# High products ahead of low ones behind seven norms, an output chunk inside the way back, and four moved steps, in a two-block transformer kernel

## The reference, cut to what matters

```python
def modulate(x, g_pre, shift, scale):
    return rms_norm(x, g_pre) * (1 + scale) + shift
def residual_add(x, y, g_post, gate, res_w):
    return x + res_w * (1 + gate) * rms_norm(y, g_post)
# first block, for each of two layers: mod = silu(c) @ ada_w + ada_b
x = residual_add(x, swiglu(modulate(x, ...), gate, up, down), ...)    # d_ff 2816
x = residual_add(x, token_mixer(modulate(x, ...), ...), ...)          # three attentions, gated sum, @ w_out
x = residual_add(x, swiglu(modulate(x, ...), gate, up, down), ...)
# second block, for each of two layers: mod = silu(c_2) @ ada_w_2 + ada_b_2
h = rms_norm(x) * (1 + sc1) + sh1
x = x + g1 * attention(h)          # layer 0: differential ("heads a"), layer 1: chunked band ("heads b")
h = rms_norm(x) * (1 + sc2) + sh2
x = x + g2 * grouped_moe(h)        # 16 experts of width 512, two per token
```

## Time and profile before

| | |
|---|---|
| median of 3 runs | 2142.19 us (2140.47 to 2143.39) |
| profiled execution, its own time | 2136.77 us |
| its span, first to last instruction | 2135.0 us |
| PE busy | 1974.8 us, 92% |
| DVE busy | 1413.3 us, 66% |
| ACT busy | 849.8 us, 40% |
| mean granted TensorE clock | 0.979 |

### The profile page before, as it was taken

One profiled execution on the slowest core, in us unless ns is written; L12 is line 12 of the kernel. 1 busy time (PEld: TensorE's weight loads), 2 busy tenths in 40 slices (PEclk: granted clock), 3 DMA queues, 4 the chain that ended last, 5 costly groups with the idle time before them and its releaser, 6 DMA issues.

```text
span 2135.0 us, 25771 instructions
## 1 busy us (share of the span) xinstructions
PE 1974.8 (92%) x9588; PEld 1440.6 (67%) x9588; DVE 1413.3 (66%) x2138; ACT 849.8 (40%) x1127; POOL 62.9 (3%) x95
## 2 busy tenths in 40 slices
PE   3999999998999999999998999998799989879998
PEld 2788777776887788778776788776544447654443
DVE  6899787766897789877876789786411146742112
ACT  3343555555343543454665444564200035321000
POOL 0000000000000000000000000110000001000000
PEclk9999999999999999999999999999899989889999
DMA  9999544436897699654443799652999986259997
GB/s 397 374 366 376 183 175 155 152 120 246 337 366 290 270 367 375 249 187 158 157 146 140 313 371 378 195 219 91 327 421 421 421 322 249 103 204 419 421 421 318
DMA packets 98175, 597.87 MB, mean 280 GB/s; under 512 B 20240, under 2 KB 23696, under 8 KB 27408
## 3 DMA queue, kind: packets, MB, share of 16 engines
q1 hardware_dynamic: 91600, 585.18, 70.4%
q10 hardware_dynamic: 6464, 11.15, 1.5%
HBM read 595.21 MB, written 1.09 MB: 279 GB/s over the span
## 4 chain that ended last, share of the span: by engine, by line
PE 74%; DVE 10%; DMA 6%; ACT 5%; issue 3%; POOL 1%; SPq 0%; DVEq 0%; ACTq 0%
PE acc L2313 11%; PE gu L2661 10%; PE acc L2317 10%; PE acc L2316 10%; PE gu L2313 7%; PE gu L2317 7%; PE gu L2316 7%; PE tr L2661 6%; PE tr L2411 3%; PE acc L2661 3%; DMA proj<-ada_stream 2%; DVE w_lo L1361 2%; ACT w_hi L699 2%; DMA stage<-wstream 2%; DMA more_proj<-wstream 1%
## 5 line engine op out<-in xcount | busy, mean ns | idle before, releaser
L1361 DVE TENSOR_TENSOR w_lo<-stage,w_hi 128x2048 fp32r<-128x2048 f32 x232 | 530.3, 2289 | 81.5 <-ACT w_hi L699 80.3
L699 ACT ACTIVATE w_hi<-stage 128x2048 fp32r<-128x2048 f32 x232 | 442.6, 1912 | 218.8 <-PE acc L2317 213.4
L2313 PE MATMUL acc<-w_hi,hT_hi 128*128 128x512 f32 (+1 forms) x736 | 305.5, 415 | 20.1 <-DVE hT_lo L2179 12.4
L1426 DVE SCALAR_TENSOR_TENSOR proj<-proj,c_row 128x1024 f32<-128x1024 f32 x240 | 291.9, 1220 | 41.5 <-DMA proj<-ada_stream 30.1
L2313 PE MATMUL gu<-w_hi,hT_hi 128*128 128x512 f32 x704 | 282.7, 402 | 21.7 <-DVE pair L1496 10.5
L2317 PE MATMUL acc<-w_hi,hT_lo 128*128 128x512 f32 (+1 forms) x736 | 291.0, 395 | 0.0
L2316 PE MATMUL acc<-w_lo,hT_hi 128*128 128x512 f32 (+1 forms) x736 | 290.5, 395 | 0.0
L2316 PE MATMUL gu<-w_lo,hT_hi 128*128 128x512 f32 x704 | 277.0, 394 | 0.0
L2317 PE MATMUL gu<-w_hi,hT_lo 128*128 128x512 f32 x704 | 277.0, 393 | 0.0
L2313 PE MATMUL acc<-w_hi,yT_hi 128*128 128x512 f32 (+1 forms) x460 | 180.9, 393 | 3.3 <-ACT proj L1141 2.7
L2313 PEld LDWEIGHTS acc<-w_hi,hT_hi 128*128 128x128 f32 x736 | 141.3, 192 | 57.9 <-DVE hT_lo L2179 15.9
(11 more groups left out here) (256 smaller groups left out, 2333.8 us busy)
## 6 DMA issues: line engine op xcount, KB each, us to landing
stage<-wstream SPq DMA_DIRECT2D x312, 1024.0 KB, 5.6
proj<-ada_stream SPq DMA_DIRECT2D x120, 1024.0 KB, 7.8
w_raw<-wstream SPq DMA_DIRECT2D x72, 1024.0 KB, 19.3
z_mix<-wstream SPq DMA_DIRECT2D x12, 1024.0 KB, 16.6
more_yT<-wstream SPq DMA_DIRECT2D x12, 1024.0 KB, 17.9
more_prob<-wstream SPq DMA_DIRECT2D x12, 1024.0 KB, 17.6
more_proj<-wstream SPq DMA_DIRECT2D x12, 1024.0 KB, 19.1
tok<-gate_rows SPq DMA_DIRECT2D x10, 512.0 KB, 5.6
```

What stands on the lines that cost most here:

```text
L699: act.activation(w_hi[:, n % PARTS, :], stage[:, n % STAGES, :], ACT.Copy).then_inc(hi_ready, 1)
L1361: dve.tensor_tensor(w_lo[:, n % PARTS, :], stage[:, n % STAGES, :], w_hi[:, n % PARTS, :].bitcast(F32), ALU.subtract).then_inc(chunk_ready, 1)
L1426: ins = dve.scalar_tensor_tensor(w, w, 1.0, c_row[:], ALU.mult, ALU.mult, accum_out=dst)
L2313: ins = pe.matmul(dst, l_hi, r_hi, start=start, stop=False, skip_group_check=True)
```

## The change

Six edits. `first_columns` waits for `hT_hi` alone, makes the eight products with it (high and low weights), and waits for `hT_lo` only ahead of the four products that need it. The residual of the second row is no longer interrupted by `rest(0)`, which follows it. `backT` makes two turns only; `out` multiplies chunk 0, high products first, makes the other two turns, and goes on. `gate_store` stands ahead of the wait for the transposes. At the experts' end both halves of the result come ahead of both halves of the next split on ScalarE; on VectorE half 1 of that split moves into norm 8 behind the root, and norm 8's own half 0 moves behind its first scalings. In heads b the last two turns stand ahead of `half(13, 1)`. (The diff's lines in the fallback for crowded experts, `moe_dense`, follow the same order and are left out here.)

```diff
@@ SyncE
                 n = n0 + 12 + 3 * (FFN_UNITS - 1)
+                gate_store(k)
                 sp.wait_ge(tr_full, ffn_turns[k])
-                gate_store(k)
                 gate_spread(k)
...
                     n = n_out + STAGES
+                    gate_store(k + 1)
                     sp.wait_ge(tr_full, turns)
-                    gate_store(k + 1)
                     gate_spread(k + 1)
@@ ScalarE, moe
                     silu(p, 1)
-                    for h in range(2):
-                        y_high(p, h)
-                        if p == PAIRS - 1 and end < n_chunks:
-                            next_high(h)
+                    y_high(p, 0)
+                    y_high(p, 1)
+                if end < n_chunks:
+                    next_high(0)
+                    next_high(1)
@@ VectorE, moe
-                    for h in range(2):
-                        y_low(p, h)
-                        if p == PAIRS - 1 and b["n"] + 3 * MOE_BLOCKS < n_chunks:
-                            next_low(b["n"] + 3 * MOE_BLOCKS, h)
+                    y_low(p, 0)
+                    y_low(p, 1)
+                if b["n"] + 3 * MOE_BLOCKS < n_chunks:
+                    next_low(b["n"] + 3 * MOE_BLOCKS, 0)
@@ VectorE, residual
-                if between:
-                    between()
@@ VectorE, norm
                     if k == 3 * DEPTH + 2:
                         dve.wait_ge(chunk_ready, b["n"])
+                        dve.wait_ge(rs_done, norm_request(b, k, 0))
+                        next_low(b["n"], 1)
                         dve.wait_ge(next_lo, 2)
                         dve.nop().then_inc(chunk_ready, 1)
...
-                    if k and chunks:
-                        if k == 3 * DEPTH + 2:
-                            dve.wait_ge(rs_done, norm_request(b, k, 0))
+                    if k and chunks and k < 3 * DEPTH + 2:
                         lo_half(b["n"] + 1, 0, split_norms.index(k) + 1)
                     scaled(0)
+                    if k == 3 * DEPTH + 2:
+                        lo_half(b["n"] + 1, 0, split_norms.index(k) + 1)
...
-                        residual(k - 1, plan[at - 1][1], 1, between=lambda: rest(0))
+                        residual(k - 1, plan[at - 1][1], 1)
+                        rest(0)
@@ TensorE, first_columns
-                        r = 2 * t + part
+                        r, n = 2 * t + part, b["n"] + part
+                        s = n % PARTS
+                        if t == 0:
+                            chunk_wait(n)
+                        pe.wait_ge(th_ready, b["th"] - 3 + r)
+                        for k in range(4):
+                            lhs = hT_hi[:, 4 * part + k, t * P:(t + 1) * P]
+                            for w in (w_hi, w_lo):
+                                pe.matmul(dst(t), lhs, w[:, s, k * 512:k * 512 + width], start=r % 2 == 0 and k == 0 and w is w_hi,
+                                          stop=False, skip_group_check=True)
                         pe.wait_ge(tr_free, b["u"] - 1 + r)
-                        columns(b["n"] + part, dst, 4 * part, 4, part == 0, part == 1, width, only=(t,))
+                        for k in range(4):
+                            ins = pe.matmul(dst(t), hT_lo[:, 4 * part + k, t * P:(t + 1) * P],
+                                            w_hi[:, s, k * 512:k * 512 + width], start=False, stop=r % 2 == 1 and k == 3,
+                                            skip_group_check=True)
+                        if t:
+                            ins.then_inc(pe_used, 1)
@@ TensorE, new: chunk 0 of out, first its 16 high products, then its 8 low ones
+            def merged(r):
+                return [tok[:, t, (2 * r + k) * P:(2 * r + k + 1) * P] for k in range(2) for t in range(NT)]
+            def high_rows(n, lhs, turned):
+                pe.wait_ge(th_ready, turned)
+                chunk_wait(n)
...
+            def low_rows(n, lhs):
...
@@ TensorE, heads (band)
-                pe.wait_ge(o_free, b["ov"] + last + 1)
-                half(13, 1, acc[:, 2, :], 0, True, False).then_inc(pe_used, 1)
                 take_turn("yT", 1, 0)
                 take_turn("yT", 1, 1)
+                half(13, 1, acc[:, 2, :], 0, True, False).then_inc(pe_used, 1)
                 copied("yT", 1, 1)
@@ TensorE, backT and out
-                    for r in range(4):
+                    for r in range(2):
...
-                    for c in range(2):
-                        pe.wait_ge(tr_free, b["u"] + c - 1)
-                        rows(b["n"] + c, of(c), c == 0, False)
+                    high_rows(b["n"], of(0), b["th"] - 3)
+                    pe.wait_ge(tr_free, b["u"] - 1)
+                    low_rows(b["n"], of(0))
+                    for r in range(2, 4):
+                        turn(b["u"] - 4 + r, merged(r))
+                    pe.wait_ge(tr_free, b["u"])
+                    rows(b["n"] + 1, of(1), False, False)
```

More of the change, by code:

```diff
@@ L886, in moe_dense @@
                 act.wait_ge(chunk_ready, end)
+                ahead(end)
                 if end < n_chunks:
+                    act.wait_ge(hi_ready, end + 1)
                     act.nop().then_inc(next_hi, 1)
-                ahead(end)
             def heads(b, hd):
@@ L1630, in moe_dense @@
                 if n0 + 3 * MOE_BLOCKS < n_chunks:
-                    for h in (1, 0):
-                        next_low(n0 + 3 * MOE_BLOCKS, h)
+                    next_low(n0 + 3 * MOE_BLOCKS, 0)
             def soft_max_in(b, a, mask, scale):
@@ L2122, in mixer, with residual @@
                     lo(n0 + MIX_CHUNKS + s_ - SLOT_HEADS)
-            def residual(k, b, t, after=None, between=None):
+            def residual(k, b, t, after=None):
                 nonlocal ups
@@ L2399, in rows @@
                         ins.then_inc(half_done, 1)
+                ins.then_inc(pe_used, 1)
+            def merged(r):
[3 more added lines that the diff above has]
+                chunk_wait(n)
+                s = n % PARTS
+                for t in range(NT):
+                    for k in range(2):
+                        for h in range(2):
+                            c = slice(k * D + h * 512, k * D + (h + 1) * 512)
+                            for w in (w_hi, w_lo):
+                                pe.matmul(acc[:, 2 * t + h, :], lhs(k, t)[0], w[:, s, c], start=k == 0 and w is w_hi, stop=False,
+                                          skip_group_check=True)
+            def low_rows(n, lhs):
+                s = n % PARTS
+                for t in range(NT):
+                    for k in range(2):
+                        for h in range(2):
+                            c = slice(k * D + h * 512, k * D + (h + 1) * 512)
+                            ins = pe.matmul(acc[:, 2 * t + h, :], lhs(k, t)[1], w_hi[:, s, c], start=False, stop=False,
+                                            skip_group_check=True)
                 ins.then_inc(pe_used, 1)
@@ L3147, in _ @@
                     pe.wait_ge(mg_ready, b["mg"])
-                    for r in range(4):
-                        turn(b["u"] + r, [tok[:, t, (2 * r + k) * P:(2 * r + k + 1) * P] for k in range(2) for t in range(NT)])
+                    for r in range(2):
+                        turn(b["u"] + r, merged(r))
                 elif kind == "out":
```

## The result

The changed kernel takes 2127.03 us (median of four runs, 2124.3 to 2127.5) against 2141.7 of the kernel before: a ratio of 0.9935, 95% interval 0.9920 to 0.9951. That is 14.7 us less, where the prediction said 8.85 and its range ended at 2128.5. The direction held and so did most of the mechanisms; the size did not. Beside the experiments the same kernel was timed twice more: 0.9922 [0.9908, 0.9936] and 0.9935 [0.9923, 0.9947].

What follows compares the result with a forecast made beforehand. TensorE, busy for 92% of the span, was taken as the bound, so gains were its idle time removed. Terms 2.7 + 2.9 + 1.6 + 1.65 = 8.85 us off the 2142.19 median gave 2133.3 us; range 2128.5 to 2140.5.

Steps and rivals of the forecast that it cites:

- The wait of 0.45 us at 514.05 goes ... Gain 0.45 us a norm: Norm 2's second row: TensorE's wait vanishes; 0.45 us taken for each of norms 1 to 6, 2.7 us.
- 512.94 stays: Norm 2: the second row's transposes start no sooner, as ScalarE's copy of row 1 still ends at 512.17.
- the bound: Norms: up to 1.0 us gain each, in mixers also because the last round's low half stops holding TensorE.
- chunk 2's cover: Out projection: chunk 2's low half is ready at 491.7, needed at 492.05, 0.35 us to spare.
- I put the same 8.85 to the median: Sum: the 8.85 us gain worked out from the profiled execution also comes off the runs' median of 2142.19 us.
- the absence: Way back: without the gate rows' earlier store, store and spread hold the residual, costing up to 4 us a place.
- the upper bound: Experts' end with norm 8: a gain of at most 2.0 us, where 1.6 was the term.
- Which the lead of 1.7 us brings forward in full: Norm 8: TensorE's first products wait for the high half only, so come the full 1.7 us sooner; term 1.6 us.
- Rival 1: Norms give nothing, set by the second row's copy; the rest holds, 6.15 us, so 2136.0 us; chance 0.19.
- Rival 3: First six sublayers: modulation weight loads take the gains back; 3.7 us left, 2138.5 us; chance 0.15.
- Rival 2: Norms: clock falls ahead of the second row, 13.6 us loss against 8.85 gain, 2146.9 us; chance 0.10.

Runs made afterwards that it cites:

- the late store: The kernel after with the gate rows' store behind the wait for the transposes again: 2139.6 us, ratio 0.9992.
- the one with filled norms: The kernel before with ten useless products ahead of the first products of norms 1 to 6 and 8: 2149.8 us, ratio 1.0033.

## Why the prediction was right in direction and short in size

By parts, from the means of the stretches over all profiles with and without each part: norms 1 to 6 5.6 us (said 2.7), the two output chunks 4.4 (2.9), the experts' end with norm 8 2.0 (1.6), the band 2.3 (1.65). The sum is 14.3, and 14.7 was measured.

**Norms: the step that failed.** "The wait of 0.45 us at 514.05 goes ... Gain 0.45 us a norm". The mechanism was right, and so was "512.94 stays". The size was not: a dense norm gives 1.09 to 1.21 us. The wait of 0.45 shown held TensorE for 0.72, and a second hold, 0.10 shown in the last round, for 0.38. The working knew of that one for the mixers alone and kept it for the bound. Three of the four dense norms gain 0.2 to 0.3 more on average, since the old order let the clock fall for longer in some executions (stretches of +0.77 to +1.07). The mixers' norms give 0.5 together, not 0.9: 1.05 each without a fall behind the second gap, a loss of 0.3 to 0.6 with one. There the new 0.4 us wait for the third chunk's low half (line 1363) stands behind the norm, which the working did not have.

**Output chunk.** At the same clock the edit is worth 1.55 to 1.6 us (said 1.45, bounds 0.8 to 1.6), and chunk 2's cover held: no product of the out projections waits for its low half. What was missing is the clock. It falls in the way back in seven of twelve old places and costs 1.6 to 2.6 us there, and in five of fourteen new ones, at 1.6 us: the old places average +1.2, the new ones -1.0. The profiled execution of before had no fall at either way back. Its mean clock was 0.979, against 0.973 in 34 other runs. So the second step that failed is "I put the same 8.85 to the median": the terms were read from an execution that lacked falls which most others have. That the edit makes falls rarer, and not only shorter, is not shown by so few places.

**Gate rows.** Right about the absence: 4.4 us of wait in the first place without it, and more by the clock. That the edit is worth nothing by itself was not run.

**Experts.** The sum came to 2.0, the upper bound, and the share was wrong. The high products first give norm 8 1.2 to 1.6 us by themselves; the reordering gives nothing alone and 0.6 to 0.9 on top. "Which the lead of 1.7 us brings forward in full" failed at the second row, whose residual stands behind the half split that was moved.

**Band.** 1.64 us of wait, 1.9 us of gain at equal clock, and the mean of 2.3 has a profile at -3.5 in it, the one profile in which the clock did not fall over the half products.

**Rivals.** Rival 1 is refuted by the four dense norms in every profile with the whole part, the late store's aside. Rival 3 too, for the dense blocks: from first transposes to first transposes the blocks behind norms 3 and 5 are 1.22 and 1.10 us shorter in the kernel after, as much as the norms themselves, unless the landing of a last transfer adds or takes 2 us. Rival 2 lives: in the mixers' norms, and in two of the four dense ones where the residual keeps its old place. The section "A second HAM failure mode: psum-queue depth-cycling" of the Trainium skill's page "TensorE: Matmul & The Clock Gate", which the prediction cites, is borne out there (0.50 to 0.52 behind the second gap) and not in the four dense norms of the kernel after.

## What to carry to other kernels

Cost a wait between pipelined products by start times (the distance to when the product would have started), not by the idle time shown: here each was some 0.28 us dearer, and one of 0.10 stood for 0.38. Take terms from more than one profile, or look first at how its mean clock stands to that of the other runs of the same kernel: what an edit saves by keeping the clock up is not in an execution in which it stayed up. Across kernels the mean clock tells less: the one with filled norms had 0.978 and was the slowest. When two orders are changed together, ask what the one protects: the high products alone kept less than half of the gain, with a fall behind the second gap in two dense norms.

## What the runs showed that was not expected

A fall of the clock costs by where it lies and how far it reaches: over a norm's first products nothing while it ended ahead of what the second row's transposes release (filling removed it, the stretch stayed), 0.8 to 1.1 us where it covered all twelve of them; over the products behind the second gap 1.5 us; in the old way back 1.6 to 2.6. With useless products in the idle time the clock stayed up in the way back of one profile, fell in the mixers' norms all the same, and where it was already down they cost 4 us.
